# Half of the modulation matrix's products move from TensorE to dot products on VectorE

## The chip, the cores and the metric

The kernel runs on one core of a Trainium2 chip. The metric is the device time of one execution in microseconds (us); the measurement compares medians of runs. Engines are named as in the profile: PE is TensorE, DVE is VectorE, ACT is ScalarE, POOL is GpSimd, SP is the engine that issues the transfers. PE's clock is given as a share: 1.00 is 2.4 GHz, 0.50 is 1.2 GHz.

## The reference

All of it is float32, for 256 tokens of width 1024. A first block modulates by a vector `c`, runs a convolution module and an MLP; a second block of two attention layers follows. The change touches the modulation, whose matrix `w_mod` is 1024 x 6144:

```python
mod = silu(c) @ w_mod + b_mod
sh1, s1, g1, sh2, s2, g2 = split(mod, 6)
h  = rms_norm(x, norm1_g) * (1 + s1) + sh1
u  = h @ w_pw1 + b_pw1                       # 1024 -> 2048
u  = a * sigmoid(gate)                       # the two halves of u
u  = dwconv(u, width 31) + b_dw              # per segment of 64 tokens
u  = silu(layer_norm(u, ln_g, ln_b))
x  = x + g1 * (u @ w_pw2 + b_pw2)
x  = x + g2 * (relu((rms_norm(x, norm2_g) * (1 + s2) + sh2) @ mlp_w1) ** 2 @ mlp_w2)
```

The scales `s1`, `s2` and shifts `sh1`, `sh2` are needed by channel on partitions (columns), since the normed input is transposed by then; the gates `g1`, `g2` are needed as rows that every partition holds.

## The kernel before

**Weights.** All weights come as one stream of units of 1 MB (128 partitions x 2048 floats) that SP loads in a fixed order (`plan_units`). At first there are six slots; a unit's transfer waits until its slot's former unit has been read, and SP's queue is in order, so that a unit that waits holds back all behind it. The order in the part at issue is: mod(2,0), pw1(1) part 3, pw2 part 0, mod(2,1), mod(2,2), pw2 part 1, mod(2,3), mod(4,0), mod(3,0), pw2 part 2, mod(4,1), mod(3,1), pw2 part 3, mod(4,2), mod(3,2), mod(4,3), mod(3,3), two units of the MLP's `w1`, mod(5,0) to mod(5,3). mod(v, q) is a quarter q (256 columns) of vector v; v is 0 for `s1`, 1 for `sh1`, 2 for `g1`, 3 for `sh2`, 4 for `s2`, 5 for `g2`. mod(3,1) takes the slot that pw2's part 1 leaves.

**Big products.** Each operand is split into a high and a low part (float32r), and a product is three matmuls. ACT writes the high part of a weight unit (`hi`, L588), DVE the rest (`lo`, L1048); both go through their own lists in order (`feed`). The unit's slot is free when `lo` is done.

**Modulation.** `quarters(m)` (L1698) multiplies a mod unit by `silu(c)` on PE into four partial rows; ACT copies them (`quarter_copy`, L645); PE sums them into columns (`column_sums`, L1715: two matmuls for the scale's group, two for the shift's) or a row (`row_sum`, L1730 with the bias row L1731); DVE finishes the columns (`columns`, L1122 to L1126) and ACT copies the rows (`row_copy`). The four quarters of `g1` are different: DVE adds them up over the eight k-blocks (`partial_sums`, L1186 and L1190) and PE only sums over partitions.

**The order of the work.** It is written out by hand for each engine. PE: transposes of `xs`; quarters; pw1 chunk 0 in four groups of two k-blocks, each of which needs its own scale and shift (`xf` L1140, `xl` L1146 on DVE, `xh` on ACT); pw1 chunk 1; the convolution as small matmuls (`modes` L1770, `tokens` L1777); `normal_T` (transposes of the layer norm's output); quarters(14) and (15); the four parts of pw2, each for two blocks of tokens, with quarters and column sums between; then the residual on DVE (L1259, L1262), the transposes `mid_T`, and the MLP (L1968 its first product). DVE's row between the convolution's last products and the norm: `gated(1)` (L1155), the `lo` of pw2's part 1, `filtered(1)` (L1164), statistics, `xs` (L1220), the columns.

Of the kernel before, what the change touches and what calls it, by code (L numbers as in the profile page):

```python
# [14 lines left out]
P = 128  # L15
# [65 lines left out]

def plan_units():
# [71 lines left out]
    at, split, plain, landed, holder = 0, 0, 0, [0] * EARLY_SLOTS, [None] * EARLY_SLOTS  # L154
    for i, u in enumerate(units):
# [21 lines left out]
MODS = [u for u in UNITS if not u["split"]]  # L177
LOW_IN_TWO = [u["s"] for u in SPLIT if (u["stage"][0], u["n"], u["part"]) in (("mla", 0, 1), ("sb", 0, 0), ("gu", 0, 1), ("gate", 0, 3))]

MOD_BANKS = [4, 5] * GROUPS + [1] * 4 + [7, 6, 2, 3, 4, 5, 7, 4] + [0] * 4  # L180
SUM_AT = [(6, 0)] * GROUPS + [(3, QUARTER)] + [(6, 0)] * 3
SPLIT_ROWS = (8, 9, 10, 11)
ROW_UNITS = (8, 9, 10, 11, 20, 21, 22, 23)
COLUMN_UNITS = ((0, 1), (2, 3), (4, 5), (6, 7), (12, 13), (14, 15), (16, 17), (18, 19))
# [5 lines left out]
def copies(m):  # L190

    return m + 1 if m < SPLIT_ROWS[0] else m + 1 - len(SPLIT_ROWS)

# [19 lines left out]
ROWS = ("b_mod2", "b_mod5", "b_pw2", "b_pw1a", "b_pw1g")  # L213
# [5 lines left out]
V_END = 9 * KT  # L219
# [5 lines left out]
def build(nc, stream, x, p_t, vectors, rows, rel, consts, dft_tables, taps, tap_bias, out):  # L225

    ctx = ExitStack()
    with ctx:
# [55 lines left out]
        def carve(table, start=0, limit=16512):  # L284
            views, at = {}, start
            for name, size in table:
# [6 lines left out]
                     ("stage", 4 * QUARTER), ("sel", P), ("sel1", 1), ("csb", KT * 32), ("g1", D), ("g2", D),  # L293
# [30 lines left out]
        padded_taps = one["g2"][0:TAP_ROWS, :]  # L324
        tap_rows = one["g2"][0:TAPS, :]
# [38 lines left out]
        skew = nc.dram_tensor("skew", (HD, P * 3 * P), F32, kind="Internal").ap()  # L364
        rel_dram = nc.dram_tensor("rel_dram", (HD, HOT), F32, kind="Internal").ap()
# [117 lines left out]
        def _(sp):  # L483
            def weights(units):
                for u in units:
                    old = u["before"]
                    if old:
# [3 lines left out]
                        else:  # L491
                            if old["m"] in SPLIT_ROWS:
                                sp.wait_ge(S["partial_done"], SPLIT_ROWS.index(old["m"]) + 1)
# [28 lines left out]
            sp.dma_start(rb, rel).then_inc(S["in_rel"], 16)  # L522
# [53 lines left out]
        def _(act):  # L576
# [1914 lines left out]
```

## Time and profile before

| | |
|---|---|
| median of 3 runs | 1031.82 us (1031.65 to 1034.67) |
| the profiled execution: its own time, its span | 1034.53 us, 1032.7 us |
| busy: PE, DVE, ACT | 97%, 58%, 49% of the span |
| mean granted clock of PE | 0.994 |
| read from HBM | 193.61 MB |

The span runs from the first to the last instruction; the time holds some 2 us more around it. The chain that ended last is followed back from the last instruction, at each step to what released it. Only the first 144 us are touched by the change.

### The profile page before, as it was taken

The numbers are of one execution on the slowest core, as the hardware profiler recorded it, in microseconds if no ns is written. First come the engines' busy times: TensorE is split into PE (matmuls) and PEld (weight loads), VectorE is DVE, ScalarE is ACT, GpSimd is POOL, SyncE is SP. The second block draws the span as 40 slices with busy tenths as digits, with TensorE's granted clock in tenths as the row PEclk, the third lists the DMA queues.
The fourth block names the chain that finished last, engine by engine and source line by source line (L and its number), as shares of the span: only waits on it lengthen the run. The fifth ranks groups of instructions, "written<-read, shape, count | busy, mean of one in ns | idle before, by whom it ended". The sixth has DMA issues, their size and how long they took to land.

```text
span 1032.7 us, 13807 instructions
## 1 busy us (share of the span) xinstructions
PE 1002.6 (97%) x5782; PEld 843.5 (82%) x5782; DVE 603.2 (58%) x730; ACT 506.6 (49%) x639; POOL 23.7 (2%) x47
## 2 busy tenths in 40 slices
PE   8998999999998999999999999999999999999996
PEld 6665779999997999878888888889988788888885
DVE  3587355444447639955555455764796655545465
ACT  4443455444555545654444444554565643444453
POOL 0000000000000000000000000000000100000000
PEclk9999999999999999999999999999999999999998
DMA  9967597555505544046555555436233554555531
GB/s 344 418 254 285 212 379 255 214 186 188 211 22 191 215 145 164 27 155 221 200 182 185 202 172 211 165 126 236 90 115 123 176 210 175 203 171 196 191 115 42
DMA packets 30648, 195.57 MB, mean 189 GB/s; under 512 B 3571, under 2 KB 5672, under 8 KB 9592
## 3 DMA queue, kind: packets, MB, share of 16 engines
q1 hardware_dynamic: 30586, 194.68, 52.0%
q8 instruction: 46, 0.75, 0.3%
q14 instruction: 16, 0.13, 0.0%
HBM read 193.61 MB, written 2.04 MB: 189 GB/s over the span
## 4 chain that ended last, share of the span: by engine, by line
PE 82%; DVE 11%; issue 3%; ACT 3%; DMA 1%; POOL 0%; DVEq 0%; SPq 0%; POOLq 0%; ACTq 0%
PE ps L1593 58%; PE ps L1968 9%; PE ps L2024 5%; DVE lo L1048 3%; ACT hi L588 1%; PE ps L1698 1%; PE ps L2272 1%; PE ps L2154 1%; PE ps L2108 1%; DVE scratch L1385 1%; DVE scratch L1451 1%; PE ps L1715 1%; PE ps L1777 1%; DVE scratch L1402 1%; DMA h<-x 0%
## 5 line engine op out<-in xcount | busy, mean ns | idle before, releaser
L1048 DVE TENSOR_TENSOR lo<-raw,hi 128x2048 fp32r<-128x2048 f32 (+5 forms) x140 | 310.3, 2219 | 234.8 <-ACT hi L588 234.7
L588 ACT ACTIVATE hi<-raw 128x2048 fp32r<-128x2048 f32 (+4 forms) x140 | 263.8, 1888 | 127.0 <-PE ps L1593 105.5
L1593 PE MATMUL ps<-hi,xh 128*128 128x512 f32 (+2 forms) x704 | 276.3, 392 | 9.3 <-DVE xl L1089 4.3
L1593 PE MATMUL ps<-lo,xh 128*128 128x512 f32 (+2 forms) x704 | 269.7, 383 | 0.0
L1593 PE MATMUL ps<-hi,xl 128*128 128x512 f32 (+2 forms) x704 | 269.4, 383 | 0.0
L1593 PEld LDWEIGHTS ps<-hi,xh 128*128 128x128 f32 x704 | 132.4, 188 | 46.3 <-issue 14.2
L1593 PEld LDWEIGHTS ps<-lo,xh 128*128 128x128 f32 x704 | 132.4, 188 | 25.2
L1593 PEld LDWEIGHTS ps<-hi,xl 128*128 128x128 f32 x704 | 132.7, 189 | 22.3
L1593 PE MATMUL ps<-hi,gh 128*128 128x512 f32 (+2 forms) x328 | 125.1, 382 | 0.0
L1593 PE MATMUL ps<-lo,gh 128*128 128x512 f32 (+2 forms) x328 | 124.6, 380 | 0.0
L1593 PE MATMUL ps<-hi,gl 128*128 128x512 f32 (+2 forms) x328 | 124.6, 380 | 0.0
L1968 PE MATMUL ps<-xh,hi 128*128 128x256 f32 x256 | 72.6, 284 | 0.8 <-DVE xl L1227 0.8
L1968 PE MATMUL ps<-xh,lo 128*128 128x256 f32 x256 | 72.4, 283 | 0.0
L1968 PE MATMUL ps<-xl,hi 128*128 128x256 f32 x256 | 72.4, 283 | 0.0
L1593 PEld LDWEIGHTS ps<-hi,gh 128*128 128x128 f32 x328 | 61.6, 188 | 11.6 <-issue 0.7
L1593 PEld LDWEIGHTS ps<-lo,gh 128*128 128x128 f32 x328 | 61.6, 188 | 11.2
L1593 PEld LDWEIGHTS ps<-hi,gl 128*128 128x128 f32 x328 | 61.6, 188 | 10.9
L2024 PE MATMUL ps<-xh,hi 128*128 128x256 f32 x192 | 55.3, 288 | 0.9 <-DVE lo L1048 0.7
L2024 PE MATMUL ps<-xl,hi 128*128 128x256 f32 x192 | 54.3, 283 | 0.0
L2024 PE MATMUL ps<-xh,lo 128*128 128x256 f32 x192 | 54.3, 283 | 0.0
L1968 PEld LDWEIGHTS ps<-xh,hi 128*128 128x128 f32 x256 | 49.1, 192 | 1.7 <-issue 1.3
L1968 PEld LDWEIGHTS ps<-xl,hi 128*128 128x128 f32 x256 | 49.1, 192 | 0.2
(248 smaller groups left out, 1063.2 us busy)
## 6 DMA issues: line engine op xcount, KB each, us to landing
raw<-stream SPq DMA_DIRECT2D x142, 1024.0 KB, 4.9
scratch<-stream SPq DMA_DIRECT2D x22, 1024.0 KB, 6.2
raw<-stream SPq DMA_DIRECT2D x4, 1020.0 KB, 4.9
raw<-stream SPq DMA_DIRECT2D x4, 896.0 KB, 5.9
raw<-stream SPq DMA_DIRECT2D x2, 864.0 KB, 4.5
raw<-stream SPq DMA_DIRECT2D x2, 768.0 KB, 4.5
raw<-stream SPq DMA_DIRECT2D x2, 680.0 KB, 5.0
h<-x SPq DMA_DIRECT2D x2, 512.0 KB, 4.5
```

Source lines behind the costliest of these rows:

```text
L588: nc.scalar.activation(hi[:, u["s"] % SPLIT_SLOTS, 0:n], raw_of(u, n), ACT.Copy).then_inc(S["hi_done"], 1)
L1048: nc.vector.tensor_tensor(lo[:, slot, first:n], raw_of(u, n)[:, first:n], hi[:, slot, first:n].bitcast(F32), ALU.subtract).then_inc(S["lo_ ...
L1385: nc.vector.scalar_tensor_tensor(out=work[b], in0=r[:, k, :], scalar=iw[:, b, head:head + 1], in1=in1, op0=ALU.mult, op1=ALU.add).then_inc ...
L1402: nc.vector.match_replace(work[b], top8[:, b, :], work[b], TAKEN).then_inc(S["topk_step"], 1)
L1451: nc.vector.tensor_scalar(pm[b][:, hh, :], pm[b][:, hh, :], row_inv[:, c:c + 1], None, ALU.mult).then_inc(S["m_norm"], 1)
L1593: ins = nc.tensor.matmul(out, l, r, start=start and i == 0, stop=stop and i == 2, skip_group_check=skip)
L1698: ins = nc.tensor.matmul(ps[32 * j:32 * j + 32, MOD_BANKS[m], 0:QUARTER], csb[:, k, :], w[:, k, :], start=step == 0, stop=step == 1)
L1715: ins = nc.tensor.matmul(ps[:, bank, at:at + 1], stage[:, m % 4, k * P:(k + 1) * P], one["sel1"], start=True, stop=True)
L1777: ins = nc.tensor.matmul(ps[SEG * i:SEG * (i + 1), 2 * b + c, :], dft[0:MODES + CHUNKS, G_AT + SEG * c:G_AT + SEG * (c + 1)], yb[0:MODES + ...
L1968: ins = nc.tensor.matmul(out_, w[:, k, cs], a[:, kk, :], start=(kk == 0 and c % 2 == 0 and i == 0), stop=(kk == KT - 1 and i == 2), skip_g ...
L2024: ins = nc.tensor.matmul(ps[:, bank + c // 2, (c % 2) * SEQ:(c % 2 + 1) * SEQ], w[:, k, cs], a[:, kk, :], start=(kk == 0 and c % 2 == 0 an ...
L2108: nc.tensor.matmul(ps[:, bank, at % 512:at % 512 + nk], qT[0:QK, hh, b * P:(b + 1) * P], kT[0:QK, hh, 0:nk], start=True, stop=False, skip_ ...
```

## The change

Twelve of the 24 mod units are stored transposed: all of `s1` (v 0), all of `g1` (v 2), and quarters 2 and 3 of `s2` (v 4) and `sh2` (v 3). Such a unit holds for each of 128 output channels, on a partition, two times 1024 weights; DVE multiplies them by `silu(c)` laid along the row (`crow`) and sums up in the same instruction (`accum_out`), which gives two columns a unit. These twelve need neither quarters, copies, column sums nor row sums. `crow` is made at the start: DVE builds eight diagonal blocks (1024 columns), PE multiplies them by ones in two matmuls of 512 columns, ACT copies the result. `g1` comes out as columns; DVE adds the bias, SP writes the 1024 values to DRAM and reads them back as a row for every partition. Beside this DVE's `feed` of pw2's part 1 moves from behind `gated(1)` to behind `xs`, and the feeds of pw2's parts 2 and 3 get two dot units behind each.

```diff
+DOTS = {(0, 0), (0, 1), (0, 2), (0, 3), (2, 0), (2, 1), (2, 2), (2, 3), (4, 2), (3, 2), (4, 3), (3, 3)}
...
+            sp.wait_ge(S["gate_done"], 1)
+            sp.dma_start(gate_dram.rearrange("(p j) -> p j", p=P), one["gate"]).then_inc(S["gate_dma"], 16)
+            sp.wait_ge(S["wave_ps"], CHUNKS)
+            sp.wait_ge(S["gate_dma"], 16)
+            sp.dma_start(one["g1"], gate_dram.partition_broadcast(P)).then_inc(S["gate_dma"], 16)
...
+            def dots(v, q):
+
+                at = dotted(v, q)
+                u = DOT_UNITS[at // 2]
+                dve.wait_ge(landed[u["slot"]], u["landed"])
+                w = raw_of(u, SLOT).rearrange("p (i k) -> p i k", i=2)
+                for i in range(2):
+                    nc.vector.scalar_tensor_tensor(out=w[:, i, :], in0=w[:, i, :], scalar=1.0, in1=crow, op0=ALU.mult, op1=ALU.mult,
+                                                   accum_out=dot[:, at + i:at + i + 1]).then_inc(S["dot_done"], 1)
...
+                dots(0, i)
+                scale_columns(i)
                 if i == 0:
                     feed(units_of(("pw1", 0))[i], 0)
-                columns(i)
-                dve.wait_ge(S["cols_done"], 2 * (i + 1))
+                shift_columns(i)
...
             gated(0)
             feed(units_of(("pw1", 1))[2], 0)
-            partial_sums(0)
+            dots(2, 0)
...
             gated(1)
-            feed(units_of("pw2")[1], 0)
             filtered(1, 0, 1, 2, 3)
...
-            columns(4)
+            feed(units_of("pw2")[1], 0)
+            scale_columns(4)
+            shift_columns(4)
...
-            columns(5)
+            scale_columns(5)
+            shift_columns(5)
             feed(units_of("pw2")[2], 0)
-            columns(6)
+            dots(4, 2)
+            dots(3, 2)
             feed(units_of("pw2")[3], 0)
+            dots(4, 3)
+            dots(3, 3)
+            for g in (6, 7):
+                scale_columns(g)
+                shift_columns(g)
             feed(units_of("w1", 0)[0], 0)
-            columns(7)
             feed(units_of("w1", 0)[1], 0)
...
+            for i in range(2):
+                ins = nc.tensor.matmul(ps[:, 4 + i, :], one["ones"], one["stage"][:, i * CHUNK:(i + 1) * CHUNK], start=True, stop=True)
+            ins.then_inc(S["xnT_ps"], 1)
...
                 elif at == 2:
                     pe.wait_ge(S["silu_done"], KT)
                     column_sums(5)
-                    quarters(16)
-                elif at == 3:
-                    quarters(17)
-                elif at == 4:
-                    column_sums(6)
-                    quarters(18)
-                elif at == 5:
-                    pe.wait_ge(S["quarter_sb"], copies(16))
-                    quarters(19)
-                elif at == 6:
-                    column_sums(7)
```

PE's quarters are renumbered with it: what was quarters(15), of mod(3,1), is quarters(7) now.

The rows below show DVE's order at the end of the convolution, from `gated(1)` to `xs`, first before and then in the changed kernel (an `x` at the end counts repeats; `waits` names the semaphores).

```order
L1155 TENSOR_TENSOR scratch<-ps,scratch 128x512 [waits sig_done] x2
L1048 TENSOR_TENSOR lo<-raw,hi 128x2048 [waits hi_done]
L1164 TENSOR_TENSOR scratch<-ps,scratch 120x512 [waits conv_ps,modes_ps] x4
L1169 BN_STATS scratch<-ps 128x6 [waits conv_ps]
L1173 BN_AGGR scratch<-scratch 128x2 [waits stats_done]
L1175 TENSOR_SCALAR scratch<-scratch 128x1 [waits ln_aggr]
L1169 BN_STATS scratch<-ps 128x6 [waits conv_ps]
L1173 BN_AGGR scratch<-scratch 128x2 [waits stats_done]
L1175 TENSOR_SCALAR scratch<-scratch 128x1 [waits ln_aggr]
L1217 SCALAR_TENSOR_TENSOR scratch<-scratch 128x1 [waits ln_rstd]
L1220 TENSOR_SCALAR xs<-ps,scratch 128x1024 [waits ln_rstd]
```

```order
L1214 TENSOR_TENSOR scratch<-ps,scratch 128x512 [waits sig_done] x2
L1223 TENSOR_TENSOR scratch<-ps,scratch 120x512 [waits conv_ps,modes_ps] x4
L1228 BN_STATS scratch<-ps 128x6 [waits conv_ps]
L1232 BN_AGGR scratch<-scratch 128x2 [waits stats_done]
L1234 TENSOR_SCALAR scratch<-scratch 128x1 [waits ln_aggr]
L1228 BN_STATS scratch<-ps 128x6 [waits conv_ps]
L1232 BN_AGGR scratch<-scratch 128x2 [waits stats_done]
L1234 TENSOR_SCALAR scratch<-scratch 128x1 [waits ln_aggr]
L1261 SCALAR_TENSOR_TENSOR scratch<-scratch 128x1 [waits ln_rstd]
L1264 TENSOR_SCALAR xs<-ps,scratch 128x1024 [waits ln_rstd]
L1068 TENSOR_TENSOR lo<-raw,hi 128x2048 [waits hi_done]
```

The `lo` that stood between the gate's products and `filtered(1)` now stands behind `xs` (L1220, now L1264).

The next rows show DVE's order from the `lo` of pw2's part 2 on, before up to the residual (L1259), then in the changed kernel up to the columns of group 6.

```order
L1048 TENSOR_TENSOR lo<-raw,hi 128x2048 [waits hi_done]
L1122 TENSOR_TENSOR scratch<-ps,scratch 128x2 [waits col_sums]
L1123 TENSOR_TENSOR scratch<-ps,scratch 128x2
L1126 TENSOR_TENSOR scratch<-scratch 128x2 [waits sum_in]
L1048 TENSOR_TENSOR lo<-raw,hi 128x2048 [waits hi_done] x2
L1122 TENSOR_TENSOR scratch<-ps,scratch 128x2 [waits col_sums]
L1123 TENSOR_TENSOR scratch<-ps,scratch 128x2
L1126 TENSOR_TENSOR scratch<-scratch 128x2 [waits sum_in]
L1048 TENSOR_TENSOR lo<-raw,hi 128x2048 [waits hi_done]
L1259 TENSOR_TENSOR xs<-ps,scratch 128x512 [waits pw2_ps,row_evac]
```

```order
L1068 TENSOR_TENSOR lo<-raw,hi 128x2048 [waits hi_done]
L1148 SCALAR_TENSOR_TENSOR scratch<-scratch 128x1024 [waits landed4]
L1148 SCALAR_TENSOR_TENSOR scratch<-scratch 128x1024
L1148 SCALAR_TENSOR_TENSOR scratch<-scratch 128x1024 [waits landed5]
L1148 SCALAR_TENSOR_TENSOR scratch<-scratch 128x1024
L1068 TENSOR_TENSOR lo<-raw,hi 128x2048 [waits hi_done]
L1148 SCALAR_TENSOR_TENSOR raw,scratch<-raw,scratch 128x1024 [waits landed0]
L1148 SCALAR_TENSOR_TENSOR raw,scratch<-raw,scratch 128x1024
L1148 SCALAR_TENSOR_TENSOR raw,scratch<-raw,scratch 128x1024 [waits landed1]
L1148 SCALAR_TENSOR_TENSOR raw,scratch<-raw,scratch 128x1024
L1163 TENSOR_TENSOR scratch<-scratch 128x2 [waits dot_done]
L1166 TENSOR_TENSOR scratch<-scratch 128x2 [waits in_sum]
```

Eight dot instructions (L1148) are put in, two units behind each `lo`, and the columns of groups 6 and 7 follow them all.

The last rows show SP's queue from pw2's part 2 on: the loads into the slots of mod(2,1) and mod(2,2) (`x2`), then that of mod(3,1), which waits for the `lo` of pw2's part 1, pw2's part 3, and the units mod(4,2) and mod(3,2) (`x2`).

```order
L498 DMA raw<-stream 128x2048 [waits partial_done] x2
L498 DMA raw<-stream 128x2048 [waits lo_done]
L498 DMA raw<-stream 128x2048 [waits partial_done]
L498 DMA scratch<-stream 128x2048 [waits mod_used] x2
L498 DMA raw<-stream 128x2048 [waits lo_done]
L498 DMA raw<-stream 128x2048 [waits mod_used] x2
```

```order
L515 DMA raw<-stream 128x2048 [waits dot_done] x2
L515 DMA raw<-stream 128x2048 [waits lo_done]
L515 DMA raw<-stream 128x2048 [waits dot_done]
L553 DMA gate_dram<-scratch 128x8 [waits gate_done]
L556 DMA scratch<-gate_dram 128x1024 [waits gate_dma,wave_ps]
L515 DMA scratch<-stream 128x2048 [waits mod_used] x2
L515 DMA raw<-stream 128x2048 [waits lo_done]
L515 DMA raw<-stream 128x2048 [waits mod_used] x2
```

The gate's write and its read are put between pw2's part 3 and mod(4,2).

## Rows read from the trace of the kernel before

**Rows 1.** The page's chain that ended last: shares of the span by engine.

```profile
PE 82%; DVE 11%; issue 3%; ACT 3%; DMA 1%; POOL 0%; DVEq 0%; SPq 0%; POOLq 0%; ACTq 0%
```

**Rows 2.** The chain in order of time: start us, us, what; 0 to 260.

```profile
20.37 2.90 PE ps L1593 x6
...
30.94 1.63 PE ps L1593 x6
...
49.69 2.96 PE ps L1593 x12
...
56.65 1.13 PE ps L1742 x4
...
75.89 0.43 PE ps L1730 x2
76.32 0.31 PE ps L1731
...
84.00 2.96 PE ps L1593 x12
...
88.22 0.40 DVE lo L1048
...
91.75 3.58 PE ps L1777 x8
...
103.22 2.94 PE ps L1593 x12
...
109.77 0.79 PE ps L1715 x8
...
131.42 0.69 DVE xs L1259
...
135.66 0.70 PE ps L1730 x2
...
144.22 5.99 PE ps L1968 x48
```

**Rows 3.** Windows: length; PE, PEld, DVE, ACT, POOL busy; clock, DMA share, GB/s.

```profile
20.30:23.70 3.40, 3.33 (x14) 2.10 (x18) 0.00 (x0) 0.00 (x0) 0.00 (x0) 0.51 1.09 340
24.00:57.00 33.00, 32.66 (x198) 21.88 (x187) 14.81 (x23) 16.50 (x20) 0.00 (x0) 1.00 1.01 414
57.00:87.00 30.00, 30.00 (x126) 21.02 (x125) 28.29 (x48) 10.62 (x12) 0.00 (x0) 1.00 0.67 250
89.50:91.70 2.20, 0.00 (x0) 0.00 (x0) 2.20 (x4) 0.00 (x0) 0.00 (x0) 1.00 0.26 34
92.00:95.00 3.00, 3.00 (x8) 0.46 (x4) 1.96 (x5) 0.00 (x0) 0.12 (x1) 0.50 0.92 374
```

**Rows 4.** TensorE's timeline: start us, us, instruction; one quarter product.

```profile
29.62 1.07 PE L1698 MATMUL ps<-raw,scratch 128*32 128x256 f32 x16
```

**Rows 5.** Groups by form, DVE and ACT: busy us, mean ns | idle before.

```profile
L1190 DVE SCALAR_TENSOR_TENSOR scratch<-raw,scratch 128x256 f32<-128x256 f32 x28 | 13.6, 485 | 1.0
...
L1347 DVE SCALAR_TENSOR_TENSOR h<-h,rstd,gain 128x1024 f32<-128x1024 f32 x2 | 2.5, 1279 | 0.0
...
L677 ACT ACTIVATE scratch<-ps 128x1024 f32<-128x1024 f32 x2 | 2.0, 1024 | 2.0 <-PE ps L1803 2.0
...
L601 ACT ACTIVATION_READ_ACCUMULATOR xs<-h 128x1 f32 x4 | 0.7, 186 | 0.0
```

**Rows 6.** DVE's timeline: start us, us, instruction [idle before <-releaser].

```profile
45.61 0.16 DVE L1122 TENSOR_TENSOR scratch<-ps,scratch 128x2 f32<-128x2 f32 x1 [5.70 <-PE ps L1715]
...
97.17 1.34 DVE L1220 TENSOR_SCALAR xs<-ps,scratch 128x1024 f32<-128x1024 f32 x1 [0.60 <-POOL scratch L1004]
...
129.21 2.29 DVE L1048 TENSOR_TENSOR lo<-raw,hi 128x2048 fp32r<-128x2048 f32 x1 [0.86 <-ACT hi L588]
```

**Rows 7.** DMA issues from 90.4 to 90.7: KB, us from issue to landing.

```profile
raw<-stream SPq DMA_DIRECT2D x1, 1024.0 KB, 4.8
```

**Rows 8.** DMA issues of the whole span, one that writes to DRAM.

```profile
out<-xs SPq DMA_DIRECT2D x2, 256.0 KB, 2.2
```

More of the change, by code:

```diff
@@ L168, in plan_units @@
             split += 1
+        elif (u["stage"][1], u["n"]) in DOTS:
+            u["d"] = dots
+            dots += 1
         else:
@@ L323, in build @@
         rel_row = one["rel_row"][0:HD, :]
-        padded_taps = one["g2"][0:TAP_ROWS, :]
-        tap_rows = one["g2"][0:TAPS, :]
+        padded_taps = one["g1"][0:TAP_ROWS, :]
+        tap_rows = one["g1"][0:TAPS, :]
+        crow = one["crow"]
+        gate2 = one["crow"]
+        dot = one["dot"]
+        diagonals = one["stage"].rearrange("p (k m) -> p k m", k=KT)
         two = carve([("Z", 3072), ("X", 2304), ("Y", 2304), ("iqT", 4 * SEQ), ("ikT", SEQ), ("work", 3 * P),
@@ L754, in _ @@
                 if i == 0:
-                    row_copy(6, one["g2"])
+                    row_copy(2, gate2)
                 if i == 1:
-                    quarter_copy(23)
-            row_copy(7, one["g2"])
+                    quarter_copy(11)
+            row_copy(3, gate2)
             for j in range(MLP_CHUNKS):
@@ new lines, in shift_columns @@
+            def shift_columns(g):
+                ks = slice(GROUP_KT * g, GROUP_KT * (g + 1))
+                v, q = (1, g) if g < GROUPS else (3, g - GROUPS)
+                if (v, q) in DOTS:
+                    at = dotted(v, q)
+                    dve.wait_ge(S["dot_done"], at + 2)
+                    total = dot[:, at:at + 2]
+                else:
+                    dve.wait_ge(S["col_sums"], g + 1)
+                    bank, at = SUM_AT[g]
+                    total = ps[:, bank, at + GROUP_KT:at + 2 * GROUP_KT]
+                nc.vector.tensor_tensor(in_shift[:, ks], total, vec[:, V_SHIFT + ks.start:V_SHIFT + ks.stop],
+                                        ALU.add).then_inc(S["shift_done"], 1)
@@ L1203, in _ @@
             statistics(0, 1)
-            partial_sums(2)
-            partial_sums(3)
+            dots(2, 2)
+            dots(2, 3)
+            at = dotted(2, 0)
+            dve.wait_ge(S["dot_done"], dotted(2, 3) + 2)
+            nc.vector.tensor_tensor(one["gate"], dot[:, at:at + KT], vec[:, V_GATE:V_GATE + KT], ALU.add).then_inc(S["gate_done"], 1)
             dve.wait_ge(S["in_consts"], 32)
```

241 lines of the change are left out of this document (120 added, 121 removed).

## The prediction

> **What bounds the kernel now.** I read four views in this order: the chain's shares on the page, the chain in order of time over the first 260 us, the vector engine's timeline, and the queue's transfers. TensorE carries 82% of the chain [rows 1]. So a change pays if it shortens the chain up to the first MLP matmul, which starts at 144.22 [rows 2]; behind it nothing is edited. All the edits lie ahead of that point. The chain there is TensorE with short hand-overs to DVE: `xl` ahead of the matmuls at 30.94, `lo` at 88.22, and ACT's `hi` and DVE's `lo` ahead of the residual at 131.42 [rows 2, 6]. In this stretch DVE is no spare engine: from 57 to 87 us it is busy 28.29 of 30 us [rows 3].
>
> **What the change takes from TensorE.** A quarter product costs 1.07 us [rows 4]; eight go, 8.6 us. A pair of column sums costs 0.79 [rows 2]; four pairs are halved and two go, 3.2 us. A row sum costs 0.43 + 0.31 [rows 2]; four go, 3.0 us. That is 14.8 us of TensorE. I now walk the chain with these prices to see how much arrives at 144.22.
>
> **Price of a dot product.** The trace has no VectorE instruction with an accumulator. A SCALAR_TENSOR_TENSOR over 128x1024 f32 with two operands in SBUF takes 1279 ns, over 128x256 485 ns [rows 5]: 1.03 ns per column, both operands. Two neighbours that don't wait overlap by 0.08 (`lo` at 129.21 lasts 2.29, the next instruction starts at 131.42) [rows 2, 6], so the lower bound is 1.20. On ACT the accumulator's read-out adds an instruction of 186 ns [rows 5]. I take 1.35 per instruction, 2.7 per unit. The upper bound is two passes, the 2.29 that 2048 columns take [rows 6]. Twelve units cost 32 us of DVE, against the 13.6 of the 28 partial sums that leave (and four shorter first ones, some 15 in all) [rows 5].
> The Trainium skill, Vector Engine (DVE) Microarchitecture Reference, section Points that are easy to get wrong, says that the scalar-tensor-tensor shape with two sources in SBUF that aren't bf16 runs at half throughput, since no port is left for the accumulator's read-back. The rows without an accumulator show no halving (1.03 ns per column); the form with one is in no row. By the rule a unit would cost about 4.6, not 2.7; that is a rival below.
>
> **Step A, the start: 0.7 later.** DVE builds the diagonals ahead of `xs` (1024 columns with two operands, 1.2 by [rows 5]), TensorE multiplies 2 x 512 columns of f32 (0.43 for 256 [rows 2], so 1.7), ACT copies 1024 columns more from PSUM (1.02 [rows 5]). The second transposed copy then ends at about 13.5 instead of 11.8. DVE waits for it and does in turn dots 2.7, scale 0.4, `lo` 2.2, shift 0.2, `xf` and `xl` with ACT's `xh` between 2.0: 21.1. Before, the first pw1 matmul starts at 20.37 [rows 2].
>
> **Step B, groups 1 to 3: 2.0 back.** Of a group's quarters, the one ahead of its first matmul goes. The other stays: 1.63 for the first half [rows 2], 1.07 for the quarters [rows 4], 1.6, and 0.4 for the column sums left are 4.7. Then DVE's `xf`, `lo` and `xl` come last: 4.1 before, from the column sum's use at 45.61 to the matmul at 49.69 [rows 2, 6], 3.8 now, since the scale is there already. So groups start every 10.0 (half clock at first: 2.90 for 1.6 [rows 2]), 8.5 and 8.7 us, at 31.1, 39.6 and 48.3; the last was at 49.69. The bias matmuls start at 55.3 instead of 56.65 [rows 2]: 1.35 ahead. The dots sit in DVE's idle time between `xl` and the next column sum (5.7 us of idle before the one at 45.61 [rows 6]). The slots come free later, but the queue is full until 57 (DMA share 1.01 from 24 to 57 [rows 3]), so landings don't move.
>
> **Step C, three row sums: 2.2.** TensorE ends pw1 at 83.4, 3.5 ahead. DVE's load there falls by 15 - 10.8, so it keeps up.
>
> **Step D, the end of the convolution: 3.6.** Before, 8.4 us pass from 86.96 to 95.33 [rows 2]: row sum 0.74, then `filtered(1)` waits behind `lo` of pw2's part 1 (2.2), TensorE rests 2.2 and its clock falls to 0.50 after it, so that the eight `tokens` rows take 3.58, of which 1.7 is the clock's [rows 2, 3]. The edit moves that `lo` behind `xs` and removes the row sum. Without them 4.8 us are left; `tokens` end at 88.2, 7.1 ahead.
>
> **Step E, the moved `lo` comes back as a late transfer: -4.1, and 1.7 for the clock.** Unit mod(3,1) goes into slot 2, which holds pw2's part 1 and is freed by just this `lo`. Before, its issue at about 90.5 follows that `lo` (88.22), and it lands 4.8 later [rows 7], ahead of its quarters just before 102.6. In the changed order: `xs` ends 3.2 after the tokens (97.17 + 1.34 against 95.33 [rows 2, 6]) at 91.4, `lo` 93.65, landing 98.45. TensorE has done `normal_T`, column sums and quarters(6) by 94.6 and waits 3.8 us. Quarters(7) 1.07 and the bias row 0.66: pw2 starts at 100.2, against 103.2. Of 7.1 there are 3.0 left. Behind the rest of 2.2 the clock stood at 0.50, 1.2 GHz, as it did from 20.3 to 23.7 [rows 3]; the like of it costs 1.7 again. So column_sums(5) ends at 109.25 instead of 110.56.
> Queued behind quarters(7) on ACT is pair 2 of the SiLU (quarter_copy(7)); its `xl` is needed only at 109, so it is hidden. Queued behind mod(3,1) on SP are pw2's part 3, the gate's write and its read: writes to DRAM land in 2.2 [rows 8]. The gate is there by about 110, 20 us ahead of the residual: hidden. But SP waits for the write, and mod(4,2) lands at 109 too, 3 us ahead of DVE.
>
> **Step F, DVE from column_sums(5) to the residual: 0.** Before, 20.9 us pass from the end of column_sums(5) (109.77 + 0.79) to the residual at 131.42 [rows 2]; DVE has four `lo` and small sums in them, and in the end waits for ACT's `hi` (0.86 before 129.21) [rows 6], which waits for TensorE. Now DVE has one unbroken row: nine small sums of the columns and their waits 1.4, four `lo` 8.8, four dots 10.8: 21.0. The residual starts at 130.2, 1.2 ahead. TensorE is through with pw2 at 127.0 (eight blocks of 2.94, 0.66, 0.79 and the 1.7 behind 100.2 [rows 2]); its 5.6 us less of quarters and column sums in this stretch buy nothing.
>
> **Step G, the clock again: +1.0.** TensorE then rests from 127.0 to 132.2, where the third residual step is done (three of 0.69 [rows 2]), and as after the rest of [rows 3] I expect half clock behind it. Its first quarters are covered by ACT's squares until 134.4 (135.66 less 1.2 [rows 2]); from there row_sum, quarters and `mid_T` set the pace. A half-clocked stretch of 3.4 us, as long as the one from 20.3 to 23.7 [rows 3], that starts with the work or up to 2 us later reaches 1.3 to 3.4 us past 134.4 and costs half of that, 0.6 to 1.7; I take 1.0.
>
> Sum: +0.7 - 2.0 - 2.2 - 3.6 + 4.1 + 1.7 + 0.1 + 1.0 = -0.2 at 144.22. The profiled execution took 1034.53 for a span of 1032.7, 2.7 above the median of 1031.82, and is at the upper end of the runs; 1.8 of it lies outside the span. I apply the difference to the median: 1031.6.
>
> **Rivals.**
> 1. The clock stays up and the accumulator is free. Then E and G lose 2.7 us less, and the dots at 1.20 take 1.2 off F and 0.3 off A: -4.4, 1027.4. For it: the price per column of [rows 5] leaves no hint of an extra pass. Against it: the rest of 2.2 in [rows 3] is shorter than those to come, and 0.50 followed it. 0.18.
> 2. A dear read-out, 1.65 per dot. Eight of them stand in F (+2.4), two in A (+0.6), and the middle has no room for 0.5 more: about +3.4, 1035. From there on the change is slower by more than 0.3%. Nothing in the trace excludes it. 0.17.
> 3. Two passes, 2.29 per dot, 1.9 more per unit: A +1.9; in each group dots end 0.5 behind the column sum, +1.5; in the middle DVE is full already and gets 18.4 instead of 15.6, so the convolution ends 7 later than forecast; F +7.6. Together +14, 1046. It decides from 1.65 per dot on, as rival 2. 0.10. The Trainium skill's sentence told above (Vector Engine (DVE) Microarchitecture Reference, Points that are easy to get wrong) would end here if it holds for this form.
> 4. The transfers move and nothing else: if mod(3,1) were there in time, pw2 would start at 96 and F end at 124. I give this no chance of its own, since the wait for `lo_done` stands in the queue's order; a part of it is in rival 1.
>
> **How the numbers follow.** The forecast has 0.55, with its own range 1028.5 to 1034.5. No change means within 0.3% (3.1 us), about what runs here can tell apart. Faster: rival 1 and 0.04 of the forecast, 0.22. Slower: rival 3, 0.13 of rival 2 and 0.05 of the forecast, 0.28. Same: 0.50. The range 1025.5 to 1037.5 leaves out rival 3 and tails of about 0.05 on either side.
>
> **What would show it.** In the changed profile: dots at 1.35 (F, rivals 2 and 3); first pw1 matmul at 21.1; bias of chunk 1 at 55.3; tokens end at 88.2 with no half clock there; TensorE waiting near 95 to 98.5 for `raw` before quarters(7), and half clock after it; pw2 from 100.2; no DVE idle between 109 and 130; residual at 130.2; first L1968-type matmul near 144. The prediction is wrong if the dot costs more than 1.6, if TensorE doesn't wait for mod(3,1), or if a stretch behind 144 changes its length.

## The result, and the profile after

| | before | after |
|---|---|---|
| median (14 runs each) | 1033.23 us (1031.65 to 1036.20) | 1037.20 us (1035.37 to 1040.69) |
| profiled execution: time, span | 1034.53, 1032.7 us | 1040.42, 1038.6 us |
| mean granted clock of PE | 0.994 | 0.982 |
| first MLP matmul starts at | 144.22 us | 150.06 us |

The ratio is 1.0037 [1.0026, 1.0048]: the changed kernel is slower by 4 us. In the profiled executions it is 5.9 us, and 5.84 of them are there at the first MLP matmul. The time less that start is 890.3 us before and 890.4 after: the loss lies in the part that was edited. The profiled execution of after is one of its longest, and has the lowest mean clock of the 14: 0.982, where the other 13 have 0.984 to 0.988. Its steps are read below and show where the time goes; how much there is of it in a usual execution is told by the medians alone.

The page of after: the grant of TensorE's clock in 40 slices (26 us each), and the shares of the chain. Slice 1 reads 8 and slice 6 (130 to 156 us) reads 7; before, all but the last read 9.

```profile
PEclk8999979999999999999999999999999999999998
PE 79%; DVE 12%; issue 3%; ACT 3%; DMA 2%; POOL 0%; SPq 0%; DVEq 0%; POOLq 0%; ACTq 0%
```

The chain of after in order of time (start us, us, what), against [rows 2]. PE's share fell from 82% to 79%, yet the first pw1 matmul stands at 22.96, not 20.37, and the transfer of a weight unit (`raw<-stream`) stands in the chain twice.

```profile
22.96 2.90 PE ps L1645 x6
...
58.38 1.13 PE ps L1793 x4
...
89.69 1.10 PE ps L1828 x4
...
93.96 2.21 DVE lo L1068
96.18 4.69 DMA raw<-stream
...
101.01 1.94 PE ps L1750 x16
...
104.09 4.62 PE ps L1645 x12
...
112.32 0.80 PE ps L1769 x8
...
122.58 7.45 DMA raw<-stream
130.05 1.92 ACT hi L612
...
134.20 0.69 DVE xs L1311
...
150.06 5.98 PE ps L2002 x48
```

The `tokens` rows end at 90.79 (95.33 before): the convolution is 4.5 ahead there. Then the `lo` of pw2's part 1, the transfer of mod(3,1) and quarters(7) stand one behind the other, all 16 rows of quarters in 1.94 instead of 1.07.

Windows of after (length; busy PE, PEld, DVE, ACT, POOL; clock, DMA share, GB/s). The stretches at clock 0.50, that is 1.2 GHz, are the first, second, fourth and last; before they were 3.4 us at the start and about as much at the tokens (3.0 of it in the window of [rows 3]). Here they sum to 30 us.

```profile
15.50:18.80 3.30, 3.30 (x21) 2.73 (x23) 3.23 (x5) 0.15 (x1) 0.00 (x0) 0.50 1.00 417
22.40:29.00 6.60, 6.04 (x25) 3.58 (x26) 3.03 (x7) 1.21 (x2) 0.00 (x0) 0.50 1.02 353
97.20:100.80 3.60, 0.00 (x0) 0.00 (x0) 1.27 (x2) 1.92 (x4) 0.00 (x0) 1.00 0.88 341
100.90:107.60 6.70, 6.59 (x26) 3.99 (x27) 1.39 (x2) 4.53 (x8) 0.00 (x0) 0.50 0.54 212
131.60:145.10 13.50, 8.33 (x46) 4.20 (x46) 8.88 (x11) 3.70 (x8) 1.48 (x4) 0.50 1.01 419
```

What TensorE did ahead of each is in its timeline (start us, us, instruction [idle before <-releaser]). It was idle (a rest, from here on) for 1.29, 2.33, 3.89 and 6.69 us. The second row is the counterpart of the first matmul of [rows 2], before which it had been idle for 1.47 in the kernel before.

```profile
14.00 0.47 PE L1793 MATMUL ps<-gh,gl 36*128 36x512 f32 x1 [1.29 <-ACT scratch L706]
22.96 0.77 PE L1645 MATMUL ps<-hi,xh 128*128 128x512 f32 x1 [2.33 <-DVE xl L1205]
101.01 0.66 PE L1750 MATMUL ps<-raw,scratch 128*32 128x256 f32 x4 [3.89 <-DMA raw<-stream]
136.27 0.66 PE L1750 MATMUL ps<-scratch 128*32 128x256 f32 x4 [6.69 <-DVE xs L1311]
```

DVE's timeline of after: one dot product with its read-out, the next one, and the last two `lo` ahead of the residual. A dot starts every 1.15 us; a unit costs 2.3.

```profile
115.68 1.22 DVE L1148 SCALAR_TENSOR_TENSOR scratch<-scratch 128x1024 f32<-128x1024 f32 x1
116.83 0.08 DVE L1148 DVE_READ_ACCUMULATOR scratch<-scratch 128x1 f32 x1
116.83 1.22 DVE L1148 SCALAR_TENSOR_TENSOR scratch<-scratch 128x1024 f32<-128x1024 f32 x1
...
127.82 2.29 DVE L1068 TENSOR_TENSOR lo<-raw,hi 128x2048 fp32r<-128x2048 f32 x1
131.99 2.29 DVE L1068 TENSOR_TENSOR lo<-raw,hi 128x2048 fp32r<-128x2048 f32 x1 [1.88 <-ACT hi L612]
```

SP's timeline of after: the write of the gate, its read 6.92 later, and behind it mod(4,2), whose first dot is the one at 115.68, on time.

```profile
97.03 0.43 SPq L553 DMA_DIRECT2D gate_dram<-scratch  x1
103.95 0.33 SPq L556 DMA_DIRECT2D scratch<-gate_dram  x1
104.32 0.91 SPq L515 DMA_DIRECT2D scratch<-stream  x2
```

### The profile page after: what moved, and what is told of

Same layout as the page of the kernel before. It is cut to its first block, busy times and chain, and to the rows that moved or that the text cites. A ratio compares the mean times of both kernels' runs of the same rounds, so it can differ in the third digit from the quotient of the medians.

```text
span 1038.6 us, 13473 instructions
## 1 busy us (share of the span) xinstructions
PE 996.4 (96%) x5614; PEld 839.7 (81%) x5614; DVE 618.0 (60%) x748; ACT 503.8 (49%) x628; POOL 24.5 (2%) x47
## 4 chain that ended last, share of the span: by engine, by line
PE 79%; DVE 12%; issue 3%; ACT 3%; DMA 2%; POOL 0%; SPq 0%; DVEq 0%; POOLq 0%; ACTq 0%
PE ps L1645 56%; PE ps L2002 9%; PE ps L2058 5%; DVE lo L1068 3%; DMA raw<-stream 2%; ACT hi L612 1%; PE ps L1750 1%; PE ps L2306 1%; PE ps L2188 1%; PE ps L2142 1%; DVE scratch L1437 1%; DVE scratch L1503 1%; DVE scratch L1454 1%; DMA table<-consts 0%; PE ps L2209 0%
```

## The experiments

**The theory:** the work terms of the prediction are right, and the loss is TensorE's half clock behind rests that the change makes longer, much more of it than forecast, together with the late transfer of mod(3,1). **Rivals:** the dots load DVE and that sets the residual; the moved `lo` is a gain on balance and the clock alone loses; the gate's way through DRAM holds up the queue.

All ratios are to the kernel before, run beside it on the same chip in five rounds, with the 95% interval; the medians are of 5 to 12 executions and come from several chips, so the ratios are what to compare. A ratio of 0.0010 is 1.03 us. "MLP" is the start of the first MLP matmul in the profiled execution. "Dummies" are additions to `keep_busy(n)`: n products of 128 columns whose result nobody reads; they change no output.

| run | what differs from the changed kernel | median us | ratio | MLP |
|---|---|---|---|---|
| e1 | dummies at three places | 1029.45 | 0.9952 [0.9939, 0.9965] | 139.11 |
| e6 | dummies at the start alone | 1036.14 | 1.0025 [1.0016, 1.0034] | 145.87 |
| e13 | ahead of quarters(7) alone | 1035.37 | 1.0020 [1.0006, 1.0034] | 147.43 |
| e7 | 24 behind pw2 alone | 1035.60 | 1.0022 [1.0010, 1.0034] | 147.86 |
| e15 | 30 behind pw2 alone | 1035.46 | 1.0016 [1.0006, 1.0026] | 145.95 |
| e14 | start and ahead of quarters(7) | 1031.38 | 0.9982 [0.9972, 0.9991] | 141.20 |
| e2 | `lo` ahead of `gated(1)` | 1029.45 | 0.9954 [0.9936, 0.9972] | 139.21 |
| e5 | `lo` behind `gated(1)`, as before | 1033.59 | 0.9998 [0.9987, 1.0009] | 143.69 |
| e3 | w1's second `lo` behind the residual | 1035.33 | 1.0004 [0.9992, 1.0016] | 146.51 |
| e4 | last eight dots over 8 columns | 1036.04 | 1.0017 [1.0008, 1.0027] | 146.12 |
| e17 | no way through DRAM | 1038.58 | 1.0040 [1.0025, 1.0055] | 148.20 |
| e9 | e2, dummies at the start, 24 behind pw2 | 1030.07 | 0.9951 [0.9933, 0.9969] | 139.44 |
| e10 | e9 with 10, and e3's edit | 1025.55 | 0.9911 [0.9898, 0.9925] | 135.07 |
| e16 | e9 with 32 | 1025.99 | 0.9929 [0.9917, 0.9941] | 135.81 |
| e8 | kernel before, dummies 8 and 20 | 1034.34 | 1.0005 [0.9997, 1.0014] | 143.82 |
| e11 | kernel before, dummies 8 and 9 | 1033.53 | 0.9996 [0.9986, 1.0006] | 141.96 |
| e12 | kernel before, 8, and `lo` ahead of `gated(1)` | 1034.13 | 1.0007 [0.9995, 1.0019] | 144.07 |

In every profiled execution but those of e9 (891.3) and e11 (891.6), the time less MLP is 890.0 to 890.5 us.

**e1: no half clock.**

```diff
+            keep_busy(5)
             pe.wait_ge(S["pick_done"], 3)
...
             column_sums(0)
+            keep_busy(8)
...
             pe.wait_ge(S["shift_done"], 5)
+            keep_busy(14, 0)
             quarters(7)
...
+            keep_busy(24)
             pe.wait_ge(S["res_step"], 3)
             quarters(8)
```

> The changed kernel with dummy matmuls in TensorE's rests: 5 before the first bias matmuls, 8 behind the first column sums, 14 before quarters(7), 24 behind pw2. Nothing else is edited. Theory (half clock behind the longer rests makes the change slower): clock 1.00 from 20 to 150 us, first MLP matmul at 143 to 145 instead of 150.06, time about 1032 (0.3% under the changed kernel's 1037.2, within 0.2% of the kernel before). Rival (the late transfer and the dot products alone make it slower): clock up, but the MLP starts at 148 or later and the time stays at 1036 or more.

Measured 1029.45, 2.6 us better than expected, and MLP at 139.11 instead of 143 to 145. Windows of it: the clock is at 1.00 throughout.

```profile
6.80:20.00 13.20, 11.80 (x92) 9.25 (x90) 11.21 (x19) 6.76 (x9) 1.82 (x3) 1.00 1.00 411
20.00:96.00 76.00, 72.12 (x397) 48.66 (x395) 56.87 (x87) 32.93 (x38) 1.10 (x2) 1.00 0.80 311
96.00:139.00 43.00, 39.68 (x261) 30.07 (x261) 27.82 (x42) 17.31 (x26) 1.48 (x4) 1.00 0.90 360
```

Its chain, for the table in the next section:

```profile
53.90 1.13 PE ps L1793 x4
...
85.21 1.10 PE ps L1828 x4
...
91.70 4.82 DMA raw<-stream
...
98.29 2.95 PE ps L1645 x12
...
104.85 0.80 PE ps L1769 x8
...
126.31 0.70 DVE xs L1311
...
139.11 5.99 PE ps L2006 x48
```

Products that nobody reads make the changed kernel 0.0085, 8.8 us, faster. The transfer still takes its 4.82 behind the `lo`. So the clock is the larger part, and with it kept up the change is a gain of 5 us over the median before. That median has half clock of its own, though: the 28 executions of the kernel before, on record with these runs, whose mean clock was 0.997 or more took 1031.59 to 1032.81. Against those the gain is 2 to 3 us.

**e2 and e5: where the `lo` of pw2's part 1 stands.** e5 undoes this one edit; e2 goes the other way.

```diff
 # e2 (e5: between the two lines)
+            feed(units_of("pw2")[1], 0)
             gated(1)
             filtered(1, 0, 1, 2, 3)
...
-            feed(units_of("pw2")[1], 0)
             scale_columns(4)
```

> The changed kernel with one edit on DVE: the lo of pw2's part 1 stands before gated(1) instead of behind xs. Theory (that lo frees mod(3,1)'s slot, so its place makes the transfer late): mod(3,1) lands before 92, TensorE's rest of 3.89 us before quarters(7) and the half clock behind it are gone, pw2 starts at about 97 to 99 instead of 104.1, the residual 5 to 7 us earlier; half clock behind pw2 stays. Time 1030 to 1032. Rival (the transfer is late for DRAM or queue reasons, such as the gate's write): pw2 still starts at 103 or later, time as the changed kernel, 1037.

> The changed kernel with one edit undone: the lo of pw2's part 1 stands behind gated(1) again, where the kernel before has it. My theory (the moved lo gives step D and takes it back as step E, with the half clock behind the wait): tokens end about 3.5 later than in the changed kernel (94.3 instead of 90.77), mod(3,1) is issued near 88 and has landed by 93, TensorE doesn't wait for raw ahead of quarters(7), no half clock there; pw2 starts at 102 to 102.5 instead of 104.09 and column_sums(5) end at 109.5 to 110 instead of 113.12. The half clock at the start and behind the residual stays. Ratio to before 1.0037 less 0.003, so 1.0005 (0.999 to 1.002). Rival (the moved lo is a gain on balance, and the loss is all from the half clock at the start and behind pw2): ratio 1.0037 or above, up to 1.006.

The chain of e5: the tokens rows wait and take 3.56 again as in [rows 2], and pw2 starts at 100.96, 3.1 ahead of the changed kernel.

```profile
89.53 3.56 PE ps L1828 x8
...
100.96 2.94 PE ps L1645 x12
...
107.51 0.80 PE ps L1769 x8
...
143.69 5.99 PE ps L2002 x48
```

Undoing the moved `lo` gives back 0.0039, all of the loss: what the moved `lo` gives in step D is smaller than what it takes in E. The rival (a gain on balance) is out. With the `lo` a place earlier than before both the rest at the tokens and the late transfer go: 0.0083. A part of e2's lead in the profile isn't its edit's: its start is that of the changed kernel and has the same rests (1.29 and 2.33), but half clock for 3.4 us only. e2's windows, at the start and ahead of pw2:

```profile
15.00:20.80 5.80, 3.04 (x33) 2.18 (x32) 5.03 (x10) 1.65 (x4) 0.00 (x0) 1.00 1.01 422
21.00:24.40 3.40, 3.40 (x14) 1.96 (x18) 2.35 (x6) 0.00 (x0) 0.00 (x0) 0.50 1.03 311
93.00:96.00 3.00, 3.00 (x38) 1.64 (x38) 1.08 (x4) 2.80 (x6) 0.00 (x0) 1.00 0.99 395
```

**e3 and e4: DVE ahead of the residual.** In the first the `lo` of w1's second unit goes behind the residual's additions; in the second the eight dots of `s2` and `sh2` run over 8 of 1024 weights, so that quarters 2 and 3 of these vectors are not computed.

```diff
 # e4
-                    nc.vector.scalar_tensor_tensor(out=w[:, i, :], in0=w[:, i, :], scalar=1.0, in1=crow, op0=ALU.mult, op1=ALU.mult,
+                    n = 8 if v > 2 else D
+                    nc.vector.scalar_tensor_tensor(out=w[:, i, 0:n], in0=w[:, i, 0:n], scalar=1.0, in1=crow[:, 0:n], op0=ALU.mult, op1=ALU.mult,
```

> The changed kernel with one edit on DVE: the lo of w1's second unit stands behind the residual adds. Theory (the residual waits for DVE's row, whose last piece is the wait for that unit's transfer, ACT's hi and this lo): the residual starts at about 130 instead of 134.2, TensorE's rest behind pw2 shrinks from 6.7 to about 2.5 us, the half-clocked stretch behind it is shorter; MLP start 4 to 6 us earlier, time 1031 to 1033. Rival (TensorE's own work sets the stretch): below 1 us of gain, 1036 or more.

> The changed kernel with the dot products of the four units of v 3 and v 4 over 8 of their 1024 weights, so that quarters 2 and 3 of s2 and sh2 are not computed. It takes about 8.8 us off DVE between column_sums(5) and the residual. If the dots' own time held the residual back, it starts 8.8 earlier, at 125.4. My theory: another 4 to 5 us at most, since w1's second unit then waits for its transfer and ACT's hi: residual at 129 to 130.5, time 1032 to 1034. Rival (DVE's load is irrelevant there, the clock and the transfer are all): below 1 us.

e4 takes 9.2 us of DVE away (eight times 1.15), and gains 0.0020, 2.1 us, where 3 to 5 were expected. Its chain shows why: the residual then waits for the transfer of w1's second unit, 9.77 us in a full queue, and for the `hi` and `lo` behind it.

```profile
117.22 9.77 DMA raw<-stream
...
131.18 0.69 DVE xs L1312
```

e3 takes that wait away and gains 0.0033, 3.4 us (4 to 6 were expected), less than the 4.45 us by which its residual (129.75) is ahead in the profile: it went on at half clock.

```profile
132.10:142.30 10.20, 9.19 (x58) 4.58 (x54) 6.59 (x8) 3.64 (x8) 2.66 (x4) 0.50 1.00 414
```

**e6, e13, e7, e15, e14: the clock's price by place.**

> The changed kernel with 5 and 8 dummy products in TensorE's two rests ahead of the first pw1 matmul, and nowhere else. My theory: the half clock at 15.5 to 18.9 and 22.3 to 29.1 is gone, the first pw1 matmul starts at 20.7 as in the first of these runs and the bias matmuls at 56.0 instead of 58.38; the waits for mod(3,1) and behind pw2 stay with their half clock: ratio 1.0037 less 0.0023, 1.0014 (1.0003 to 1.0025). Rival (the transfers set the pace up to 57 us, so a faster start is lost again): bias matmuls stay near 58 and the ratio at 1.0037.

> The changed kernel with 24 dummy products in TensorE's rest ahead of the quarters behind pw2, and nowhere else. My theory: no half clock between 130 and 145, and from the residual to the first MLP matmul 12.8 to 13.3 us instead of 15.86: ratio 1.0037 less 0.003, 1.0007 (0.9995 to 1.002). Rival (this half clock lies beside ACT's squares and DVE's xl and costs little): 15 us or more between the two and a ratio of 1.003 or above.

> The changed kernel with 14 dummy products ahead of quarters(7), where TensorE waits for mod(3,1), and nowhere else. My theory (each place has its own price): no half clock near 101, pw2 opened 1.1 earlier and column_sums(5) end 3.0 earlier relative to the issue of mod(3,1); half clock at the start and behind pw2 stays: ratio 1.0037 less 0.003, 1.0007 (0.9995 to 1.002). Rival (this place is the whole remainder of what all three gave): 0.998 or below.

> The changed kernel with 30 dummy products behind pw2 instead of 24, enough for the whole rest of 6.7 us. My theory: with 24 a rest of 1.52 was left and the clock fell to 0.50 at 136.19 all the same; without that rest it stays at 1.00, and from the residual to the first MLP matmul 12.8 us pass: ratio 1.0037 less 0.003, 1.0007 (0.9995 to 1.002). Rival (the rests of 0.5 to 1.1 us behind the quarters are enough for half clock): half clock again and a ratio of 1.002 or above.

> The changed kernel with the dummies at the start and ahead of quarters(7), without those behind pw2. My theory (the prices add): 1.0037 less 0.0012 less 0.003, so 0.9995 (0.998 to 1.001), and half clock behind pw2 as in the changed kernel. Rival (the places depend on each other, and two of them give most of what three give): 0.997 or below.

By the ratios: 0.0012 for the start, 0.0017 ahead of quarters(7), 0.0015 (24) or 0.0021 (30) behind pw2, but 0.0055 for the first two together and 0.0085 for all three. The prices don't add up, though not by far more than the noise: 0.0055 exceeds the sum of its two parts by 0.0026, and the four intervals together leave that uncertain by some 0.0022. Each alone is less than was expected of it. What the profiles show is that the stretch behind pw2 has no fixed length: 13.7 us in the changed kernel, 10.2 in e13 and in e14, so what a place costs depends on where the others left the work. Why the start is worth so much more beside the middle than alone, no run here tells. The stretches also differ between executions where no edit does: at the start of the changed kernel, with the same rests of 1.29 and 2.33, the profiles have half clock for 10 us (after, e4, e5, e13, e15), some 7 (e7) or 3.4 (e2). So one profile doesn't price a place. In e7 the dummies left 1.52 us of rest, and half clock came 2 us after it; in e15, with 30, a rest of 0.63 was left, and one of 0.84 just ahead of the MLP, and the clock stayed (windows of e7, then of e15):

```profile
132.80:134.20 1.40, 0.00 (x0) 0.00 (x0) 1.36 (x3) 0.00 (x0) 0.00 (x0) 1.00 1.01 427
136.30:143.00 6.70, 6.52 (x30) 3.73 (x30) 2.71 (x4) 1.94 (x5) 1.43 (x4) 0.50 1.00 413
```

```profile
129.50:136.00 6.50, 6.50 (x65) 6.29 (x67) 5.04 (x7) 1.49 (x2) 0.00 (x0) 1.00 1.01 422
136.10:145.90 9.80, 8.37 (x88) 4.51 (x77) 4.48 (x7) 6.18 (x15) 1.48 (x4) 1.00 1.00 415
```

From the residual (133.15 in e15) to MLP it takes 12.80 us there, as before, against 15.86: step G's price in the profile of after is 3.06, all of it clock; by e15's ratio it is 0.0021, 2.2 us.

**e9, e16, e10: what the change can give.**

> The changed kernel with the lo of pw2's part 1 ahead of gated(1), and dummy products in TensorE's rests at the start (5 and 8) and behind pw2 (24). My theory (the late transfer and the half clock are separate losses): from 139.21, where the first MLP matmul starts with the early lo alone, go some 1.7 at the start and 2.5 behind the residual: 135.0, and since every profiled time so far is this start plus 890.3, 1025.3 us, ratio 0.9915 (0.990 to 0.993). Rival (the transfers' rate bounds the stage once the clock is up, so the two gains overlap): first MLP matmul at 138 or later, ratio 0.994 to 0.995 as either alone.

> The changed kernel with the lo of pw2's part 1 ahead of gated(1), the dummies at the start, and 32 behind pw2 (24 left a rest of 1.82, and half clock from 127.84). My theory: clock 1.00 up to the MLP, first MLP matmul at 136.3 instead of 139.44: 1026.7 us, ratio 0.993 (0.992 to 0.9945). Rival (the rest of 1.1 behind the first quarters brings the half clock back): first MLP matmul at 139, ratio 0.995.

> As the run before, and the lo of w1's second unit behind the residual adds (10 dummy products behind pw2 instead of 24). My theory: the last lo no longer waits for its unit to land, TensorE's rest shrinks to 2.5 us and the first MLP matmul starts at 133 (132 to 134.5): ratio 0.9895 (0.988 to 0.9915). Rival (the moved lo holds up squares' partner xl and its unit then comes late for the MLP): 0.9915 or above, with a new wait behind the first MLP matmul.

e9 missed by 4.8 us (half clock from 127.9 to 134.6, behind a rest of 1.82; and 1 us more behind the MLP, where ACT's `hi` waits 4.16 us for a transfer ahead of the first attention product, 2.93 in e16). With eight dummies more the half clock is gone, and e16 came out at 1025.99 for 1026.7 expected. e16 beside e1, both at full clock up to the MLP, gives the late transfer's own price: 0.0023, 2.4 us. e10, 1025.55, has the lowest ratio, 0.9911, though its interval meets e16's; its MLP start is 135.07 for 133 expected, and its profile still has half clock behind the residual's start.

**e8, e11, e12: the kernel before with the same means.**

> A control: the kernel before with 8 dummy products ahead of its first pw1 matmul and 20 ahead of the tokens rows of chunk 1, the two places where its profile has half clock. My theory: 1.3 us less at the start and 1.7 at the tokens rows, so ratio 0.997 (0.996 to 0.998), which is less than the 0.0085 that dummies gave the changed kernel; the change would be ahead of before by about 0.0015 when neither has half clock. Rival (dummies do something else that speeds any kernel, as landing times or a power state): 0.993 or below; other rival (the rests are covered by other work): 0.999 to 1.001.

> The control again with fewer dummies: the kernel before with 8 dummy products ahead of its first pw1 matmul and 9 instead of 20 ahead of the tokens rows of chunk 1 (20 ran to 92.95, 2.4 past the end of the wait, and ate the gain). My theory: tokens end at 92.4 instead of 95.33, first MLP matmul at 141.3 instead of 144.22 and a ratio of 0.9975 (0.9965 to 0.9985). Rival: the half clock of the kernel before costs its median run nothing (its profiled run is one of the slower): 0.999 to 1.000.

> The kernel before with 8 dummy products ahead of its first pw1 matmul and the lo of pw2's part 1 ahead of gated(1). This asks whether the gain of the early lo needs the dot products. My theory: DVE is full up to 87 us there (28.29 of 30 us busy), so the lo only moves the wait to modes, and the tokens end 0 to 1.7 earlier by this edit: with the start's 1.3 a ratio of 0.998 (0.9965 to 0.999). Rival (DVE has the room, and the early lo is a gain of any kernel): tokens end 5 us earlier than 95.33, ratio 0.995.

None of the three gained: 0.997, 0.9975 and 0.998 were expected, and e8 and e11 came out in the range of a rival (the rests are covered by other work; half clock costs the median nothing). So dummies by themselves don't make a kernel faster. That half clock is free here isn't shown, though: the kernel before's own executions with the fullest clock (1031.6 to 1032.8, above) are ahead of e11's 1033.5, which pays for its dummies and for the wait told below. e8 was ill-sized: the 20 dummies ran to 92.95, some 2.4 us past the time at which DVE had the first rows ready (90.5). e11 had clock 1.00 all along, its MLP start is 2.26 ahead, and its median is that of the kernel before. Of the 2.26 it lost 1.2 at the first attention product: ACT's `hi` there waits for a transfer, for 2.90 us before, 2.96 in e8 and 4.18 in e11 (ACT's timelines of the last two).

```profile
314.02 1.91 ACT L588 ACTIVATE hi<-raw 128x2040 fp32r<-128x2040 f32 x1 [2.96 <-DMA raw<-stream]
```

```profile
313.39 1.91 ACT L588 ACTIVATE hi<-raw 128x2040 fp32r<-128x2040 f32 x1 [4.18 <-DMA raw<-stream]
```

The other 1 us is the distance of the profiled execution of before from its median. In e12 the earlier `lo` made TensorE wait 1.86 us for `gated(1)` and gained nothing (MLP 144.07): DVE has no room for it in the kernel before. In the changed kernel four dot units, 9.2 us, stand ahead of it in place of partial sums of some 15; that this makes the room is argued, no run tests it alone.

**e17: the gate.** The row is read from another one that lies in DRAM, without the write; the first gate holds that row's values instead of `g1`.

```diff
-            sp.wait_ge(S["gate_done"], 1)
-            sp.dma_start(gate_dram.rearrange("(p j) -> p j", p=P), one["gate"]).then_inc(S["gate_dma"], 16)
             sp.wait_ge(S["wave_ps"], CHUNKS)
-            sp.wait_ge(S["gate_dma"], 16)
-            sp.dma_start(one["g1"], gate_dram.partition_broadcast(P)).then_inc(S["gate_dma"], 16)
+            sp.dma_start(one["g1"], rows["final"].partition_broadcast(P)).then_inc(S["gate_dma"], 16)
...
-            dve.wait_ge(S["gate_dma"], 32)
+            dve.wait_ge(S["gate_dma"], 16)
```

> The changed kernel without the gate's write to DRAM: the gate's row is read from a row that lies in DRAM since the start (another row's values, so the first gate is another vector), and SP waits for nothing there. My theory (the round trip is hidden): mod(4,2) is issued near 97.5 instead of 104.32 and lands well ahead of its use at 115.68, DVE's row from column_sums(5) to the residual is as before, ratio 1.0037 (1.0025 to 1.005). Rival (the stop in SP's queue pushes the later units together, and w1's second unit, landed at 130.03, comes late by it): the residual starts up to 1.9 earlier, which is DVE's idle time ahead of it, and the ratio is 1.002 or below.

SP issues mod(4,2) at 95.88 instead of 104.32, and then waits for DVE until 115.18 all the same:

```profile
95.88 1.15 SPq L515 DMA_DIRECT2D scratch<-stream  x2
115.18 7.11 SPq L515 DMA_DIRECT2D raw<-stream  x4
```

The ratio is 1.0040 [1.0025, 1.0055], beside 1.0037 for the changed kernel: the way through DRAM costs nothing that these runs can tell, which is about 2 us. In the profile DVE still waits 1.51 us ahead of its last `lo`, 1.88 in the changed kernel.

## Why the prediction failed

The direction failed, not the range: 1031.6 was forecast from a shift of -0.2, and the medians show +4.0. None of the signs of being wrong that the prediction gave itself came: the dot costs less than 1.6, TensorE waits for mod(3,1), and the stretch behind the MLP's start keeps its length (890.3 and 890.4). Step by step, as differences to the kernel before, in us, from the chains ([rows 2] and the rows above; e1 is the same work at full clock):

| step | from, to | forecast | after | e1 |
|---|---|---|---|---|
| A | start, first pw1 matmul | +0.7 | +2.6 | +0.3 |
| B | bias matmuls | -2.0 | -0.9 | -3.1 |
| C, D | tokens end | -5.8 | -6.3 | -6.3 |
| E, transfer | pw2 start | +4.1 | +5.4 | +4.1 |
| E, clock | column_sums(5) end | +1.7 | +1.7 | 0.0 |
| F | residual | +0.1 | +0.2 | -0.2 |
| G | first MLP matmul | +1.0 | +3.1 | 0.0 |
| sum | | -0.2 | +5.8 | -5.1 |

(In e1 the first pw1 matmul starts at 20.71.) The +5.8 is that of two single executions; 1.9 of it is that the profile of after lies 3.2 above its median, and that of before 1.3.

**What failed** is the clock's price. Step G says: "A half-clocked stretch of 3.4 us [...] costs half of that, 0.6 to 1.7; I take 1.0." The stretch was 13.7 us long and cost 3.06, above the upper end, as e15 shows. Step E priced the clock behind the wait at 1.7 by the same 3.4 us; it was 6.7 long and cost 3.0 (1.3 of it in the quarters and the opening rows ahead of pw2). And steps A and B had none beyond what the kernel before had: TensorE's rests of 1.29, behind the new `crow` products and the transposes, and of 2.33, which was 1.47, had 10 us of half clock in their train. After is 2.25 behind e1 at the first pw1 matmul and 2.2 more at the bias matmuls; 0.66 of it is no clock, since the first constants landed that much later (DVE's first copy behind them starts at 7.50, in e1 at 6.84). That leaves some 3.8 us. By the ratios the half clock of the three places costs 1.2, 1.8 and 2.2 us when each is kept up alone, and 8.8 when all are, against 2.7 forecast for the last two and nothing for the start; either sum is enough to turn the sign. I had taken the shortest length on record as the length, and had not asked what new rests the walk itself had put at the start.

**D and E together** were forecast at +2.2 with the clock (-3.6, +4.1, +1.7). D's term holds a row sum of 0.7 that e5 doesn't bring back, so for the moved `lo` alone it is +2.9; e5 measures 4 us. The direction was right, and the mechanism at its time: transfer 4.69 for 4.8, TensorE idle 3.89 for 3.8.

**What held:** the walk of the work. The same kernel at full clock (e1) is 5.1 ahead at MLP; without its clock terms (+1.7, +1.0) the forecast has -2.9. Of the difference of 2.2, the half clock that the kernel before has at its start (2.90 for the first six rows, 1.6 at full clock) and that e1 doesn't have is 1.3; the cheaper dots may be in the rest, which no run splits.

**The dot's price** was 1.15, not 1.35: below the lower bound of 1.20. The overlap with the neighbour (0.07) was in the bound; the instruction itself takes 1221 ns, not 1279, and the read-out (0.08) lies under the end of the dot and the start of the next. Rivals 2 and 3 are out. The Trainium skill's rule on the scalar-tensor-tensor shape (Vector Engine (DVE) Microarchitecture Reference, Points that are easy to get wrong) isn't borne out here: 1221 ns for 1024 columns with the accumulator, against 1279 for the same shape without [rows 5]. Cheap dots gave nothing in F, since the residual waited for w1's transfer, as the DVE row's 1.88 of idle shows; "one unbroken row" was right in its length (21.1 for 21.0) by luck: the eight dots took 1.6 less than forecast, and the wait for that transfer, which the row was to be without, put 1.88 in.

**The gate** was hidden, as forecast, as far as e17 can tell. Its write took 6.8 to land by the transfers' records, not 2.2; it was issued right behind two units of 1 MB.

**Rival 1** had 0.18 and is the kernel that e1 shows, at 1029.45 for 1027.4, once dummies hold the clock; without them the clock fell.

## What to carry to other kernels

Where removed work turns into a wait of TensorE, price the wait and then the clock behind it, and don't take the shortest stretch seen for its length: here the change was 5 us ahead of the median before while dummies held the clock, and with half clock behind rests of 1.3 to 6.7 us it was 4 behind it. A weight's split that moves later in one engine's list also frees its slot later: look for the unit that waits for that slot, and try the place ahead of the wait too, which was worth 0.0083 here, 8.6 us. A kernel whose executions spread (5.3 us here, 1.4 in e1) is worth a look at its clock before its work is changed: in the kernel before, executions at a mean clock of 0.997 or more took 1031.6 to 1032.8, those below 0.994 took 1035.8 to 1036.8. And one profiled execution is not the usual one: compare its time and mean clock with those of the others before a step is priced from it.

## What was not expected of the hardware

- Half clock came in stretches of 3.4, 6.7, 10.2 and 13.7 us. The longest began at 131.5, 2 us into a rest of 6.69, and went on for 9 us after its end. Behind 1.52 us of rest with one of 1.11 following (e7) it came too; with rests of 0.92 and 1.10 in e1 it didn't.
- The same instructions with the same rests (but for the wait for the first constants) had different stretches from execution to execution: behind 1.29 none in e2 and e7 and 3.4 us in after, around 2.33 some 7 us in after and e7 and 3.4 in e2.
- An accumulator on VectorE costs no second pass: DVE_READ_ACCUMULATOR takes 0.08 us and starts under the dot's end, and a dot of 1024 columns with it takes 1221 ns, where the same shape without took 1279 [rows 5]; on ACT the read-out takes 0.19 [rows 5].
- A write of 4 KB to DRAM took 6.8 us to land when two units of 1 MB had been issued just ahead of it, where 256 KB had taken 2.2 [rows 8] at the end of the kernel before, with the DMA share at 0.23 (1020 to 1032 us). That the units ahead made the difference is likely, not tested.
